# Two-column TensorE products given 128 moving columns in a two-layer hybrid backbone

## The chip, the cores and the metric

The kernel is one program on one NeuronCore of a Trainium2 chip. The metric is the device time of one execution in microseconds, from the median of several executions; lower is better. TensorE multiplies: a stationary operand of up to 128 x 128 is loaded (weight load, shown as PEld), then the moving columns stream past it (matmul, shown as PE). VectorE (DVE), ScalarE (ACT) and GpSimd (POOL) work beside it, and each engine takes its instructions in order and waits on semaphores for the others.

## What is computed

Two layers over 512 latent and 256 context tokens of width 1024, all in float32. Each layer modulates its input with vectors made from `silu(c) @ w_mod`, mixes tokens in four head groups, and ends in a squared-ReLU MLP. The three parts of the reference that the change touches:

```
m = silu_c @ w_mod[l] + b_mod[l]                       # modulation: 6 vectors of 1024, for c and for c_ctx
...
kk = heads(k * p['rwkv_k_k'][d])                       # keys of the RWKV group, 4 heads of 64, 2 directions
kk = kk / jnp.maximum(jnp.sqrt(jnp.sum(kk * kk, axis=-1, keepdims=True)), 1e-12)
...
bonus = ((jnp.sum(r * dirs[0][1] * r_k, axis=-1, keepdims=True)
          + jnp.sum(r * dirs[1][1] * r_k, axis=-1, keepdims=True)) * v)
```

## The kernel before

Features lie on the 128 partitions and tokens along the free dimension. A layer runs in order: the input projection (20 tiles), in which TensorE computes each product three times over split operands (`product`, L1460 through `mm`); attention by groups; the preparation of the RWKV group (a loop over n = 0 to 11 on TensorE); the RWKV scan in three steps of chunked products (s = 0, 1, 2), each with five levels of small 64-row products; the output projection; the MLP. Every engine's program is written out by hand, with semaphores between them, so the order on TensorE is the order of the code. All matmuls but the transposes and the scan's outputs go through the helper `mm`, so the profile gives them all line L1460.

Three kinds of products have only two moving columns. Each is float32, which the trace shows as two passes (a weight load and a matmul each) per product:

- `mod_columns(row, n, at)` (L1549) turns rows of the modulation into columns: 4n products of a 128 x 128 piece with `pick` (L133, filled once on VectorE at L999), two result columns each in PSUM bank `ps`. It runs with n = 4 at the start of a layer (from `modrow`, in L1568, or `next_row`, L1582), n = 2 after attention (L1721), n = 3 and n = 1 after the preparation (L1871, L1874), n = 2 ahead of the MLP (L2135): 48 products in layer 0 and 48 in layer 1, 96 in all. VectorE copies them to `modT` (L1093, L1098).
- The keys' square sums, in the preparation at n = 1 (L1853 to L1858): 24 products a layer of `rn` with two columns of the block matrix, `bd[:, 0:P:64]`. ScalarE takes the root (L829), VectorE the reciprocal (L1216), and TensorE spreads it over the partitions (`spread_heads`, at n = 3) after the products of n = 2 and n = 3.
- The bonus, in scan step s = 0 at level j = 2 (L1960 to L1966): 12 products a layer of `bonus_in` with the same two columns. ScalarE copies them to `bon` (L928).

`keep_clock(o, n)` issues n products of 512 columns whose result nobody reads. `spread_root` spreads a root over the partitions with products of 128 moving columns. `ring_row` computes a modulation row from four weight slabs. Unlike these, `head_sums` (L1606) has two moving columns too and is not part of the change.

Of the kernel before, what the change touches and what calls it, by code (L numbers as in the profile page):

```python
# [19 lines left out]
ALU = mybir.AluOpType  # L20
ACT = mybir.ActivationFunctionType
AX = mybir.AxisListType
# [5 lines left out]
P = 128  # L28
# [58 lines left out]
K_ID, K_ONES, K_BD, K_ROT64, K_ROT96 = range(5)  # L87
NKF = 5
# [22 lines left out]
def backbone(nc, xT_d, cT_d, pcol_d, constf_d, constm_d, rope_d, wmask_d, wmod_d, win_d, wout_d, w1_d, w2_d,  # L111
             uq_d, ukv_d, w2a2_d, g2_d, ln_d, smask_d, out_d):
    with ExitStack() as ctx:
        place = {}

        def sb(name, cols, dt=F32):
            place[name] = nc.sbuf_base
            return ctx.enter_context(nc.sbuf_tensor(name, [P, cols], dt))
# [10 lines left out]
        kf = sb("kf", NKF * P)  # L129
        km = sb("km", NKM, BF16)  # L130
        cT = sb("cT", KT * 2)
        silu = sb("silu", KT * 32)
        pick = sb("pick", 2)  # L133
        modT = sb("modT", DEPTH * NMOD * 2)
        gain = sb("gain", DEPTH * 4 * 16)
        omm = sb("omm", 32)
# [4 lines left out]
        ps = ctx.enter_context(nc.psum_tensor("ps", [P, 4096], F32))  # L141
# [5 lines left out]
        gains = gain[:, :].rearrange("p (l n k s) -> p l n k s", l=DEPTH, n=4, s=2)  # L147
        siluv = silu[:, :].rearrange("p (k m) -> p k m", k=KT)
        ident, ones, bd = (kf[:, k * P:(k + 1) * P] for k in (K_ID, K_ONES, K_BD))
        rot64 = kf[:, K_ROT64 * P:(K_ROT64 + 1) * P]  # L150
        rot96 = kf[0:96, K_ROT96 * P:K_ROT96 * P + 96]
        modrow = hT[:, 2 * SLAB:2 * SLAB + 2048]
# [59 lines left out]
        KS, BONUS = 3844, 2048 + 1024 + 256  # L212
# [5 lines left out]
        bonus_in = zv[:, R_K:R_K + 2, :]  # L218
# [3 lines left out]
        sg, aa, rn = wv(W_SG, 4, TOK), wv(W_A, 4, TOK), wv(W_RN, 4, TOK)  # L222
# [42 lines left out]
        s_silu = sem("s_silu")  # L265
# [719 lines left out]
        def _(dve):  # L985
            ch = Chain(dve, s_dve)
            V = nc.vector
# [8 lines left out]
            V.tensor_tensor(siluv[:, :, 0:2], siluv[:, :, 0:2], cT[:, :].rearrange("p (k s) -> p k s", s=2),  # L996
                            ALU.mult).then_inc(s_silu, 1)
            dve.wait_ge(s_const, 48)
            V.tensor_reduce(pick[:, :], ident.rearrange("p (q m) -> p m q", q=4)[:, 0:2, :], AX.X, ALU.add).then_inc(s_silu, 1)  # L999

            def gn_roots(n):

# [78 lines left out]
            for l in range(DEPTH):  # L1081
# [44 lines left out]
                for n, (where, tile) in enumerate(ROPES):  # L1126
                    if n >= 7:
                        dve.wait_ge(s_paire, 12 * l + n - 4)
                    p = 96 if where != 64 else P
# [3 lines left out]
                    o, at = turned_at(n), (W_VB if n < 7 else W_PT) + (n % 2) * LAT  # L1133
# [11 lines left out]
                for n, b0 in streams(l):  # L1145
# [24 lines left out]
                    with dve.Fori(0, n) as i:  # L1170
                        at = i * 12 + heads0
# [53 lines left out]
                for n in range(4):  # L1225
# [4 lines left out]
                    ins = V.tensor_tensor(kd[:, n, :], kd[:, n, :], zv[:, R_K + n % 2, :], ALU.mult)  # L1230
# [3 lines left out]
                for n in range(4):  # L1234
# [6 lines left out]
                    ins = V.tensor_tensor_scan(cs[:, n, :], smask, sg[:, n, :], 0.0, ALU.mult, ALU.add)  # L1241
                    if n >= 2:
# [4 lines left out]
                        ins = V.tensor_tensor(s3, s3, c3[:, :, CH - 1:CH].to_broadcast([P, TOK // CH, CH]), ALU.add)  # L1247
# [20 lines left out]
                for v, b in enumerate(BACKWARD):  # L1268
                    ins = V.tensor_tensor(cells(-1, RV + v * 512 + P, [64, 2], [256, 2], C1),
                                          cells(-1, R_R * TOK + b * P, [TOK, 2], [64, 2], C1),  # L1270
                                          cells(-1, 17 * TOK + b * P, [TOK, 2], [64, 2], C1), ALU.mult)
# [5 lines left out]
                for n in range(1, 3):  # L1277
                    ins = gain_of(l, n)
# [52 lines left out]
                for s in range(STEPS):  # L1331
# [13 lines left out]
                    for j, half in enumerate(LEVELS):  # L1345
                        m = M_STEP + 64 * j
# [36 lines left out]
                    for k in range(4 if s < STEPS - 1 else 3):  # L1383
                        x, i = k // 2, k % 2
# [73 lines left out]
        def _(pe):  # L1458
            def mm(out, lhsT, rhs, start=True, stop=True):
                return pe.matmul(out, lhsT, rhs, start=start, stop=stop)  # L1460
# [88 lines left out]
            def mod_columns(row, n, at):  # L1549

                for m in range(4 * n):
                    ins = mm(ps[:, at + 2 * m:at + 2 * m + 2], row[:, m * P:(m + 1) * P], pick[:, :])
                ins.then_inc(s_modps, 1)

            pe.wait_ge(s_silu, 3)
# [1 line left out]
            for l in range(DEPTH):  # L1557
# [268 lines left out]
                for n in range(12):  # L1826
                    if n == 6:
                        pe.wait_ge(s_kkn, 4 * l + 3)
                        ring_row(4)
                    if n >= 2:  # L1830
                        pe.wait_ge(s_rpe, 12 * l + n - 1)
                    o = (n % 2) * 1024
                    if n < 2:
                        for b in range(NB):
                            ins = pe.transpose(ps[:, o + b * P:o + (b + 1) * P], zv[:, R_V + n, b * P:(b + 1) * P], ident)
                    elif n < 10:
                        if n == 2:
                            pe.wait_ge(s_gate, 2 * l + 1)
                            pe.wait_ge(s_rtab, 64 * (l + 1))

                        c = (512 if n < 6 else 0) + ((n - 2) % 4) * P
                        for a, b in ((0, LAT), (LAT, TOK)):
                            ins = mm(ps[:, o + a:o + b], w2a2[:, c:c + P], zv[:, R_WA, a:b])
                    else:
                        for b in (range(4) if n == 10 else range(4, 6)):
                            c = o + (b % 4) * 256
                            mm(ps[:, c:c + 256], zv[:, R_GL, b * P:(b + 1) * P], g2a, True, False)
                            ins = mm(ps[:, c:c + 256], zv[0:32, R_MISC, b * P:(b + 1) * P], g2b, False, True)
                    ins.then_inc(s_rp, 1)
                    if n == 1:  # L1850

                        keep_clock(3072, 3)
                        pe.wait_ge(s_kkq, 4 * (l + 1))  # L1853
                        for m in range(4):
                            for b in range(NB):
                                c = KS + 12 * m + 2 * b
                                ins = mm(ps[:, c:c + 2], rn[:, m, b * P:(b + 1) * P], bd[:, 0:P:64])
                        ins.then_inc(s_kks, 1)  # L1858
                    if n == 3:

                        pe.wait_ge(s_krec, l + 1)
                        for m in range(4):
                            if m >= 2:
                                pe.wait_ge(s_kkn, 4 * l + m - 1)
                            for b in range(NB):
                                ins = spread_heads(2048 + (m % 2) * 1024 + b * P, 12 * m + 2 * b)
                            ins.then_inc(s_ksp, 1)
# [9 lines left out]
                for s in range(STEPS):  # L1877
# [69 lines left out]
                    for j, half in enumerate(LEVELS):  # L1947
                        for x in range(2):
                            h, o = HALF[x], 2048 * x
                            pe.wait_ge(s_tn[x], 6 * n + j + 1)  # L1950
                            for g in range(2):
                                for p in range(2):
                                    for f in range(2):
                                        for c in range(2):
                                            ins = mm(bank(c, o + g * P + (2 * p + f) * 32, [1, 32]),
                                                     cells(c, h + ABR + p * 512 + f * 256 + g * P, C1),
                                                     cells(c, h + TN + g * (256 + half) + (2 * p + f) * 64,
                                                           [2 * half, 32 // half], [1, half]))
                            ins.then_inc(s_X[x], 1)
                        if s == 0 and j == 2:  # L1960
                            pe.wait_ge(s_gate, 2 * l + 2)
                            for b in range(NB):
                                for f in range(2):
                                    ins = mm(ps[:, BONUS + b * 4 + 2 * f:BONUS + 2 + b * 4 + 2 * f],
                                             bonus_in[:, f, b * P:(b + 1) * P], bd[:, 0:P:64])
                            ins.then_inc(s_bonps, 1)  # L1966
                        for x in range(2):
                            h, o = HALF[x], 2048 * x + 1024
                            pe.wait_ge(s_Xm[x], 5 * n + j + 1)
                            if j == 0:  # L1970
                                pe.wait_ge(s_ke[x], n + 1)
                            else:
                                pe.wait_ge(s_tt[x], 4 * n + j)
                            if s == 0 and j == 2 and x == 1:
                                pe.wait_ge(s_bon, l + 1)
                            for g in range(2):
                                for p in range(2):
                                    for f in range(2):
                                        for c in range(2):
                                            ins = mm(bank(c, o + g * P + (2 * p + f) * 32, [1, 32]),  # L1980
                                                     cells(c, h + TT + g * 256 + (2 * p + f) * 64, C1),
                                                     cells(c, h + XM + g * P + (2 * p + f) * 32, [1, 32]))
                            ins.then_inc(s_Tp[x], 1)
                            if j == 1:
                                seen(x)
# [290 lines left out]
```

## Time and profile before

| | us |
|---|---|
| median of 3 executions | 2419.48 |
| lowest and highest | 2418.77, 2426.33 |
| span of the profiled execution | 2415.9 |
| TensorE matmul busy | 2223.2 (92%) |
| TensorE weight load busy | 1795.5 (74%) |
| VectorE, ScalarE, GpSimd busy | 1000.1, 676.1, 772.3 |
| mean granted TensorE clock | 0.955 |

The profile is of one execution, from its first to its last instruction. The granted clock is given as a share of full speed: 1.0 is 2.4 GHz, 0.5 is 1.2 GHz, and a value between is a mean over both. A matmul's duration holds its latency, so the cost of one in a series is read from where one group starts to where the next starts, divided by the count.

### The profile page before, as it was taken

The page shows a single profiled execution, that of the slowest core. Times are in us where ns is not written, and L with a number is a line of the kernel's source. Part 1 is how long each engine was busy: PE and PEld are TensorE (multiplying, and loading weights), DVE is VectorE, ACT ScalarE, POOL GpSimd, SP SyncE. Part 2 cuts the span into 40 slices and gives each one's busy share as a digit, 9 for nine tenths or more (in the row PEclk, how much of TensorE's full clock was granted, in tenths as well). Part 3 has the DMA queues.
Part 4 walks back from the last instruction along what each step waited for, and adds up shares of the span by engine and source line. Part 5 has one row for each costly group of instructions (what it writes and reads, how often), then busy time and mean ns, then how long its engine had stood idle before and what let it go on. Part 6 is the DMA issues. An engine that isn't in the chain of part 4 may idle for free.

```text
span 2415.9 us, 45856 instructions
## 1 busy us (share of the span) xinstructions
PE 2223.2 (92%) x19352; PEld 1795.5 (74%) x19352; DVE 1000.1 (41%) x1512; ACT 676.1 (28%) x1184; POOL 772.3 (32%) x546
## 2 busy tenths in 40 slices
PE   5999988889989899999999899988879988999997
PEld 3888566559966688888888578856649965888886
DVE  3002355475653732414142420335565655442443
ACT  3110455642222211102111221145642223221221
POOL 2332343013131223232222343235104133444443
PEclk9999999988999899999999899999978989999998
DMA  6211100110022211112113221110030023232331
GB/s 257 86 60 53 70 1 0 58 71 3 4 79 67 82 62 61 61 61 69 61 61 130 96 104 59 36 70 0 16 112 3 4 79 114 96 96 95 95 95 61
DMA packets 45412, 162.55 MB, mean 67 GB/s; under 512 B 5504, under 2 KB 5504, under 8 KB 45024
## 3 DMA queue, kind: packets, MB, share of 16 engines
q1 hardware_dynamic: 44480, 157.89, 19.3%
q0 software_dynamic: 800, 2.69, 0.3%
q8 instruction: 109, 1.79, 0.3%
q14 instruction: 23, 0.19, 0.0%
HBM read 158.46 MB, written 2.10 MB: 66 GB/s over the span
## 4 chain that ended last, share of the span: by engine, by line
PE 79%; DVE 13%; ACT 4%; issue 3%; POOL 1%; DMA 0%; SPq 0%; ACTq 0%; POOLq 0%; DVEq 0%
PE ps L1460 76%; DVE small L1160 2%; PE ps L1775 2%; DVE part_h L1058 1%; DVE hT L1051 1%; ACT flat L774 1%; DVE xT L1076 1%; DVE flat L1444 1%; ACT flat L792 1%; DVE ps L1157 1%; DVE flat L1074 1%; POOL flat L544 1%; PE ps L2036 0%; DVE part_h L1329 0%; DMA xT<-xT_dram 0%
## 5 line engine op out<-in xcount | busy, mean ns | idle before, releaser
L1460 PE MATMUL ps<-part_hi,wparts 128*128 128x512 f32 (+1 forms) x3072 | 825.0, 355 | 28.4 <-DVE part_h L1058 9.4
L1460 PEld LDWEIGHTS ps<-part_hi,wparts 128*128 128x128 f32 x3072 | 547.5, 191 | 120.8 <-DVE part_h L1058 15.7
L525 POOL TENSOR_TENSOR wparts<-flat,wparts 128x1024 fp32r<-128x1024 f32 x184 | 446.3, 2426 | 536.0 <-ACT wparts L974 530.3
L1460 PE MATMUL ps<-part_h,wparts 128*128 128x512 f32 (+1 forms) x1536 | 544.6, 355 | 0.0
L1460 PE MATMUL ps<-flat 64*64 64x32 f32 (+8 forms) x8812 | 491.6, 264 | 55.1 <-ACT flat L792 28.5
L1460 PEld LDWEIGHTS ps<-flat 64*64 64x64 f32 (+4 forms) x8812 | 380.1, 147 | 155.6 <-issue 75.9
L1460 PE MATMUL ps<-part_mlp,wparts 128*128 128x512 f32 (+1 forms) x1536 | 417.3, 358 | 16.2 <-DVE part_h L1058 11.3
L1460 PEld LDWEIGHTS ps<-part_h,wparts 128*128 128x128 f32 x1536 | 296.0, 193 | 39.3 <-issue 1.7
L1460 PEld LDWEIGHTS ps<-part_mlp,wparts 128*128 128x128 f32 x1536 | 275.5, 191 | 62.9 <-DVE part_h L1058 13.0
L974 ACT ACTIVATE wparts<-flat 128x1024 fp32r<-128x1024 f32 x112 | 118.8, 1061 | 705.1 <-PE ps L1460 705.1
L1460 PE MATMUL ps<-part_lo,wparts 128*128 128x512 f32 (+1 forms) x768 | 272.0, 354 | 0.0
L1444 DVE TENSOR_TENSOR flat<-flat 128x768 f32<-128x768 f32 (+1 forms) x64 | 160.2, 2503 | 213.3 <-ACT flat L978 213.1
L522 POOL CAST wparts<-flat 128x1024 fp32r<-128x1024 f32 x72 | 77.5, 1077 | 519.1 <-PE ps L1460 203.3
L1451 DVE TENSOR_TENSOR flat<-flat,ps 128x768 f32<-128x768 f32 (+1 forms) x64 | 52.6, 821 | 359.8 <-PE ps L1460 359.8
L1460 PEld LDWEIGHTS ps<-part_lo,wparts 128*128 128x128 f32 x768 | 145.3, 189 | 19.8
L1160 DVE TENSOR_REDUCE small<-ps 128x1 f32<-128x768 f32 (+2 forms) x126 | 102.1, 812 | 42.7 <-PE ps L1460 41.3
L720 ACT ACTIVATE flat<-ps 128x768 f32<-128x768 f32 (+1 forms) x40 | 30.8, 770 | 310.7 <-PE ps L1460 310.7
L774 ACT ACTIVATE flat<-ps,small 128x768 f32<-128x768 f32 (+2 forms) x126 | 98.8, 788 | 43.8 <-DVE small L1160 28.9
L1775 PE MATMUL ps<-kf,flat 128*128 128x128 f32 x592 | 91.0, 285 | 9.7 <-ACT flat L774 8.8
L1775 PEld LDWEIGHTS ps<-kf,flat 128*128 128x128 f32 x592 | 65.3, 142 | 33.6 <-issue 26.5
L1118 DVE RECIPROCAL small<-small 128x48 f32<-128x48 f32 x2 | 0.9, 452 | 210.0 <-ACT small L726 210.0
L792 ACT ACTIVATE flat<-ps 128x512 f32<-128x512 f32 (+1 forms) x120 | 63.7, 530 | 84.6 <-PE ps L1775 84.1
(202 smaller groups left out, 1953.5 us busy)
## 6 DMA issues: line engine op xcount, KB each, us to landing
flat<-w_dram SPq DMA_DIRECT2D x128, 512.0 KB, 3.5
flat<-wmod_dram SPq DMA_DIRECT2D x88, 512.0 KB, 5.5
flat<-win_dram SPq DMA_DIRECT2D x40, 512.0 KB, 3.5
flat<-wout_dram SPq DMA_DIRECT2D x16, 512.0 KB, 3.5
hT<-wmod_dram SPq DMA_DIRECT2D x8, 512.0 KB, 8.2
xT<-xT_dram SPq DMA_DIRECT2D x8, 384.0 KB, 6.1
flat<-rope_dram SPq DMA_DIRECT2D x2, 1024.0 KB, 5.7
out_dram<-xT SPq DMA_DIRECT2D x8, 256.0 KB, 2.0
```

Source lines behind the costliest of these rows:

```text
L522: ch.link(pool.tensor_copy(whi[q % 2], src))
L525: pool.tensor_tensor(wlo[q % 2], src, whi[q % 2], ALU.subtract).then_inc(s_used[q], 1)
L544: ins = pool.tensor_tensor(sq[:, 0, 0:t], sq[:, 0, 0:t], sq[:, k, 0:t], ALU.add)
L720: nc_.activation(zv[:, tile, 0:t], ps[:, (q % 2) * 1024:(q % 2) * 1024 + t], ACT.Copy).then_inc(s_ev, 1)
L774: nc_.activation(prob[:, h % 2, 0:w], ps[:, (h % 2) * 1024:(h % 2) * 1024 + w], ACT.Exp, bias=small[:, h:h + 1], accum_out=small[:, 16 + h ...
L792: nc_.activation(probT[:, h % 2, 0:w], ps[:, 2048:2048 + w], ACT.Copy).then_inc(s_pta, 1)
L974: nc_.activation(whi[q % 2], slab[:, q * SLAB:(q + 1) * SLAB], ACT.Copy).then_inc(s_whi, 1)
L1160: ins = V.tensor_reduce(nm, src, AX.X, ALU.max, negate=True)
L1444: ch.link(V.tensor_tensor(raw, raw, raw, ALU.mult))
L1451: V.tensor_tensor(yT[:, k, 0:t], yT[:, k, 0:t], ps[:, o:o + t], ALU.add).then_inc(s_ev2, 1)
L1460: return pe.matmul(out, lhsT, rhs, start=start, stop=stop)
L1775: ins = pe.transpose(ps[:, c:c + P], prob[:, h % 2, b * P:(b + 1) * P], ident)
```

## The change

The two moving columns become 128. For the modulation, `pick` is 128 wide and holds its two columns 64 times over. For the other two, `halves` reads the block matrix in the order of columns 0, 64, 1, 65 and so on, so the first two result columns are those of before. The result is written 128 columns wide at the old place; the next product starts two columns further and overwrites the surplus, and nobody reads what the last one leaves behind. The number of products and their order stay.

```diff
-        pick = sb("pick", 2)
+        pick = sb("pick", P)
...
+        halves = bd.rearrange("p (j i) -> p i j", j=2)
...
-            V.tensor_reduce(pick[:, :], ident.rearrange("p (q m) -> p m q", q=4)[:, 0:2, :], AX.X, ALU.add).then_inc(s_silu, 1)
+            V.tensor_reduce(pick[:, :].rearrange("p (i m) -> p i m", m=2),
+                            bass.AP(kf, K_ID * P, [[NKF * P, P], [0, 64], [1, 2], [32, 4]]), AX.X, ALU.add).then_inc(s_silu, 1)
...
-                    ins = mm(ps[:, at + 2 * m:at + 2 * m + 2], row[:, m * P:(m + 1) * P], pick[:, :])
+                    ins = mm(ps[:, at + 2 * m:at + 2 * m + P], row[:, m * P:(m + 1) * P], pick[:, :])
...
-                                ins = mm(ps[:, c:c + 2], rn[:, m, b * P:(b + 1) * P], bd[:, 0:P:64])
+                                ins = mm(ps[:, c:c + P], rn[:, m, b * P:(b + 1) * P], halves)
...
-                                    ins = mm(ps[:, BONUS + b * 4 + 2 * f:BONUS + 2 + b * 4 + 2 * f],
-                                             bonus_in[:, f, b * P:(b + 1) * P], bd[:, 0:P:64])
+                                    c = BONUS + b * 4 + 2 * f
+                                    ins = mm(ps[:, c:c + P], bonus_in[:, f, b * P:(b + 1) * P], halves)
```

## Rows read from the trace of the kernel before

**Rows 1.** The page: the TensorE clock over 40 slices (tenths), the chain by engine.
```profile
PEclk9999999988999899999999899999978989999998
...
PE 79%; DVE 13%; ACT 4%; issue 3%; POOL 1%; DMA 0%; SPq 0%; ACTq 0%; POOLq 0%; DVEq 0%
```

**Rows 2.** Two-column places by window: length, PE, PEld, DVE, ACT, POOL busy, clock, DMA.
```profile
37.20:41.90 4.70, 4.67 (x33) 4.68 (x34) 0.03 (x1) 0.00 (x0) 4.54 (x4) 0.78 0.60 211
134.11:136.70 2.59, 2.59 (x26) 2.59 (x25) 0.00 (x0) 1.66 (x2) 2.18 (x2) 1.00 0.00 0
...
472.80:482.76 9.96, 9.94 (x49) 9.94 (x49) 0.00 (x0) 3.11 (x4) 0.00 (x0) 0.53 0.45 177
...
551.36:554.13 2.77, 2.77 (x28) 2.75 (x24) 0.42 (x1) 0.00 (x0) 0.70 (x2) 1.00 0.00 0
...
1754.24:1762.20 7.96, 7.96 (x48) 7.96 (x49) 0.00 (x0) 3.08 (x4) 0.00 (x0) 0.66 0.51 202
```

**Rows 3.** By window as above: scan s = 0, s = 1, layer 1's s = 0.
```profile
554.13:576.72 22.59, 22.59 (x450) 22.40 (x452) 9.24 (x18) 1.39 (x3) 0.00 (x0) 0.62 0.01 2
605.19:619.99 14.80, 14.80 (x454) 14.62 (x454) 9.21 (x19) 1.20 (x2) 0.00 (x0) 1.00 0.01 3
1834.03:1856.62 22.59, 22.59 (x450) 22.41 (x453) 9.24 (x18) 1.39 (x3) 0.00 (x0) 0.62 0.01 2
555.30:570.30 15.00, 15.00 (x288) 15.00 (x286) 6.65 (x13) 0.00 (x0) 0.00 (x0) 0.50 0.01 3
```

**Rows 4.** The chain of waits around the bonus of layer 0: start, length, what.
```profile
548.95 29.79 PE ps L1460 x681
```

**Rows 5.** Timeline of TensorE in the preparation: start, length, what, count, idle before.
```profile
472.82 9.94 PE L1460 MATMUL ps<-kf,flat 128*128 128x2 f32 x48 [2.08 <-ACT flat L821]
482.62 5.00 PE L1460 MATMUL ps<-flat 128*128 128x512 f32 x8
487.55 5.49 PE L1460 MATMUL ps<-kf,small 128*64 128x128 f32 x96
492.97 2.85 PE L1460 MATMUL ps<-flat 128*128 128x512 f32 x8
...
1754.24 8.12 PE L1460 MATMUL ps<-kf,flat 128*128 128x2 f32 x48 [2.13 <-ACT flat L821]
1762.22 5.20 PE L1460 MATMUL ps<-flat 128*128 128x512 f32 x8
1767.35 5.49 PE L1460 MATMUL ps<-kf,small 128*64 128x128 f32 x96
```

**Rows 6.** Timeline as above: passes with 128 moving columns; a load between 512-column passes.
```profile
783.65 1.60 PE L1460 MATMUL ps<-kf,small 128*128 128x128 f32 x12 [0.74 <-DVE small L1026]
785.09 1.85 PE L1460 MATMUL ps<-pick,flat 128*128 128x2 f32 x16
...
1383.70 2.91 PE L1460 MATMUL ps<-kf,small 128*128 128x128 f32 x12
...
48.12 0.19 PEld L1460 LDWEIGHTS ps<-kf 128*128 128x128 f32 x1 [0.24 <-issue]
```

**Rows 7.** The chain of waits after the first modulation columns.
```profile
41.87 0.20 DVE modT L1098
...
58.85 1.07 DVE part_h L1058 x2
```

**Rows 8.** Timeline, as above, at four other places.
```profile
1386.72 2.19 DVE L1051 SCALAR_TENSOR_TENSOR hT<-xT,gain,ps 128x512 f32<-128x512 f32 x4 [0.69 <-PE ps L1460]
...
5.26 0.16 DVE L999 TENSOR_REDUCE pick<-kf 128x2 f32<-128x8 f32 x1
...
18.73 3.64 PE L1460 MATMUL ps<-flat,silu 128*32 128x512 f32 x16 [18.73 <-DMA flat<-wmod_dram]
...
531.82 1.56 PE L1460 MATMUL ps<-flat 64*64 64x128 f32 x24 [5.49 <-DVE flat L1274]
```

## The prediction

> **What bounds the kernel now.** I read the page first: the chain that ended last runs 79% on TensorE, and its clock line has slices at 7 and 8 tenths amid nines [rows 1]. So the question is which TensorE time is spent at the lower of its two clock levels, and whether the two-column products have a part in that. The second view is the table by window, laid on each two-column place [rows 2]; the third lays it on what follows the bonus and on the same work one scan step later [rows 3]; then the chain of waits and the timeline tell which of these places set the end [rows 4, 5, 7].
>
> The second view shows that a place of two-column products counts as 100% busy, yet three of the five places shown have a mean clock of 0.53 to 0.78: it falls to 1.2 GHz in the middle of them although TensorE never idles there [rows 2]. Where the clock is full, 24 passes take 2.59 us, 108 ns each; in layer 0's key sums 48 take 9.80 us, 204 ns each [rows 2, 5]. The weight load of 128 columns sets that pace: it is busy as long as the matmul is.
>
> The bonus is at full clock itself, 24 passes in 2.77 us [rows 2]. What comes right after it is not: from 555.3 to 570.3 us TensorE is 100% busy at 0.50. The stretch behind the bonus takes 22.59 us in layer 0 and the same in layer 1, and the like stretch of step s = 1, which has no bonus in it, takes 14.80 us at 1.00 with the same count of matmuls (450 against 454, some records missing) [rows 3]. So the kernel's small scan products keep a full clock that they find, and don't win back one that is lost. The chain runs through this stretch on TensorE alone [rows 4].
>
> **The change part by part.** 168 products change, 336 passes: 192 of modulation columns, 96 of key sums, 48 of bonus. Nothing is moved, and no wait is added or removed.
>
> *The price of a wider pass.* The nearest row is the spread of a root, 128 moving columns and a 128-column load: 12 passes from 783.65 to 785.09 us, 120 ns each with the start of the series in it; at half clock at most 2.91 / 12 = 243 ns [rows 6]. The lower bound is no extra cost (108 ns), as the load beside it takes as long anyway. A third row: a 512-column pass is spaced 0.19 + 0.24 = 0.43 us, so 128 columns stream in 0.11 us [rows 6]. I take 113 ns, near that streaming time, since it and the load run beside each other. The 64 passes after attention and ahead of the MLP, where the clock is full now, cost 64 x 5 ns = 0.3 us.
>
> *Bonus, each layer.* 24 x 113 ns = 2.7 us, as now. If the clock then stays, the stretch behind it is 22.59 - 14.80 = 7.8 us shorter, all on the chain: 15.6 us for both layers [rows 3, 4]. This is over half of the forecast. ScalarE's copy of the bonus and the second half's wait for it come at the same distance as before.
>
> *Key sums, each layer.* The place and the eight passes after it take 487.55 - 472.82 = 14.73 us in layer 0 and 1767.35 - 1754.24 = 13.11 us in layer 1; the like eight passes at full clock take 2.8 us [rows 5]. At full clock throughout it would be 48 x 113 ns + 2.8 = 8.2 us. In layer 1 the clock is full when the place begins and falls inside it (0.66), so I take the whole 4.9 us. In layer 0 it is low almost from the first pass (0.53), behind an idle time of 2.08 us that stays [rows 2, 5]; wide passes have to win it back. Between no fall (gain 6.5) and half of the passes at half clock (24 x 225 + 24 x 113 ns + 2.8 = 10.9 us, gain 3.8) I take 5.0. What is late next is the reciprocal on VectorE, which the spread waits for; it needs the sums, one root and two short operations, about 1.2 us behind the last product, and the 2.8 us of products cover it. Sum: 9.9 us.
>
> *First modulation columns of layer 0.* 32 passes in 4.6 us at clock 0.78 [rows 2] become 32 x 113 ns and a tail of 0.25, 3.9 us: 0.8 us less. VectorE copies right behind them, and the chain then stays with VectorE and ScalarE up to 58.85 us [rows 7]. The idle-filling products after it also come at the higher clock, but TensorE waits for VectorE there in the end, so only the 0.8 us counts.
>
> *The same in layer 1.* 1379.07 to 1383.70 us shrinks by 1.0 us. The spread of the root behind it goes from 2.91 to some 1.5 us [rows 6]. VectorE was ready 0.69 us before it [rows 8], so after the change VectorE is the late one: the gain is 1.0 + 0.69 = 1.7 us, not 2.4.
>
> *Modulation columns after the preparation.* 32 passes a layer, partly at low clock, but TensorE then idles 5.49 us for VectorE before the scan begins [rows 8]: nothing. If that cover were gone they would save about 1 us a layer.
>
> *The wider `pick`.* The reduction reads 512 elements instead of 8 in an operation that took 0.16 us at 5.26 us; the first matmul begins at 18.73 us, released by a transfer [rows 8]. Even a whole microsecond is hidden; uncovered it would cost that once.
>
> *The order in which the moving columns are read.* `pick` is read straight, the 144 passes with `halves` jump 256 bytes back and forth. No row of before reads 128 moving columns so. From below the bound is no cost. From above I take the nearest row in which a column costs four times as much streaming, the 512-column pass, 430 ns. I take no cost, because a float32 pass streams slowly: 0.83 ns a column against the 0.4 ns that its clock would allow.
>
> "Advanced Engine Details and Errata" of the Trainium skill, in its section on SBUF cachelines, speaks against this edit: a read stream that needs a new 16-byte line for every element pays a penalty, and this order does so. It gives no size; by it the 144 passes are dearer, and the time is that of the third or the fourth rival below. No run here has shown it yet.
>
> *Sum against the profiled execution.* 15.6 + 9.9 + 0.8 + 1.7 - 0.3 = 27.7 us; 2415.9 - 27.7 = 2388.2 us of span. The median stands 3.6 us above the span shown, so 2391.8, say 2392 us.
>
> **The rivals.**
> 1. *The clock doesn't depend on the columns.* The five places were at 100% busy anyway, and the clock fell for what lies around them. Then only the price is left: 336 passes x 0 to 12 ns, 2420 to 2424 us. For it speaks that two of five places keep 1.00; against it that in both layers the fall comes behind the bonus and never in the same work of s = 1 [rows 2, 3]. "TensorE: Matmul & The Clock Gate" of the Trainium skill, in its section "Why this matters for your kernels", says to keep TensorE busy without idle gaps, and the full clock will stay. By that rule alone this rival holds, since the two-column passes are back to back; the trace disagrees with it, with 0.50 right behind a stretch without idle time.
> 2. *The scan still loses its clock*, in one layer or both, because the bonus interrupts it at an unlucky moment. That gives back 7.8 or 15.6 us: 2400 or 2407 us.
> 3. *Jumping reads at half pace.* A `halves` pass takes 225 ns at full clock. The places with `halves` and what hangs on them cost 14.73 + 13.11 + 2 x (2.77 + 22.59 - 14.80) = 49.0 us now, and 144 x p + 2 x 2.8 after. With p = 0.225 they save 11.0 us, with 2.2 us of the rest 13.2: 2406 us. The clock is held all the same in this case.
> 4. *Slower: jumping reads at a quarter of the pace*, in the key sums and the bonus. With p = 0.43 the same formula gives 61.9 + 5.6 - 49.0 = 18.5 us lost, 2.2 gained: 2436 us. It decides above p = 0.316 us per pass, where 144 x p + 5.6 - 49.0 - 2.2 is zero.
> 5. *More than forecast*: layer 0's key sums never fall, passes cost 108 ns, and low stretches elsewhere shrink as well: 2378 to 2382 us.
>
> **How the numbers follow.** Chances: forecast 0.61 (2383 to 2399 us by the bounds of its terms), rival 1 0.08, rival 2 0.10, rival 3 0.10, rival 4 0.06, rival 5 0.05. The first mechanism has the same difference in two layers behind it, which is why it holds most. Low end 2382, so that the upper bound of layer 0's key sums and the cheaper pass are in; high end 2407, which takes in rivals 2 and 3 and leaves 1, 4 and part of 5 out. A measurement of this kernel can tell 0.3%, 7.3 us, from no change. Faster by more: forecast, rivals 2, 3 and 5, 0.86. Within: rival 1, 0.08. Slower: rival 4, 0.06.
>
> **What would show each step.** The stretch behind each bonus: about 14.8 us at 1.00; if it is still 22.6 at 0.62, the largest term is wrong. The key sums: 5.4 us in layer 1 and 5.4 to 8 in layer 0, and their eight followers 2.8 us. A pass with `halves` next to one with `pick` at full clock: both 110 to 120 ns, or the reads cost. The first modulation columns: 3.6 us. TensorE should still idle for VectorE ahead of the scan, longer than 5.5 us if those columns shrink. The prediction would be wrong as a whole if wide passes leave the clock where it is.

## The result, and the profile after

| | before | changed |
|---|---|---|
| median, us | 2419.12 (4 runs) | 2397.26 (4 runs, 2394.62 to 2400.76) |
| span of the profiled execution | 2415.9 | 2392.8 |
| mean granted clock | 0.955 | 0.967 |
| TensorE matmul busy | 2223.2 | 2200.9 |

The ratio of changed to before is 0.9902, with a 95% interval of 0.9882 to 0.9922: 19 to 29 us faster, 21.9 by the medians and 23.1 by the two spans. The clock has two levels, so the mean clocks say how much time is spent at the lower one: (1 - 0.955) x 2 x 2416 = 217 us before, (1 - 0.967) x 2 x 2393 = 158 us after. Line numbers of the changed kernel are one or two higher.

The table by window of the changed kernel, with the columns of rows 2, answers rows 2 and 3. The eight stretches are the first modulation columns, layer 0's key sums, layer 0's bonus, layer 1's key sums, the scan behind each bonus, layer 1's first modulation columns, and the four products of modulation columns ahead of layer 0's scan:

```profile
39.30:43.10 3.80, 3.77 (x33) 3.77 (x34) 0.00 (x0) 0.00 (x0) 3.72 (x3) 1.00 0.39 132
474.20:482.08 7.88, 7.88 (x49) 7.88 (x50) 0.00 (x0) 3.09 (x4) 0.00 (x0) 0.78 0.56 223
549.45:552.92 3.47, 3.47 (x29) 3.30 (x25) 0.43 (x1) 0.00 (x0) 0.00 (x0) 1.00 0.00 0
1743.38:1750.04 6.66, 6.66 (x48) 6.66 (x49) 0.00 (x0) 3.09 (x4) 0.00 (x0) 1.00 0.56 223
552.92:567.72 14.80, 14.80 (x449) 14.62 (x452) 8.76 (x18) 1.39 (x3) 0.00 (x0) 1.00 0.01 3
1820.10:1834.90 14.80, 14.80 (x449) 14.62 (x452) 8.76 (x18) 1.39 (x3) 0.00 (x0) 1.00 0.01 3
1369.31:1372.88 3.57, 3.57 (x34) 3.57 (x32) 2.10 (x3) 0.30 (x1) 3.49 (x3) 1.00 0.80 308
522.32:524.20 1.88, 1.88 (x8) 1.78 (x8) 1.88 (x3) 0.00 (x0) 0.00 (x0) 0.50 0.00 0
```

Behind each bonus the scan takes 14.80 us at 1.00, where it took 22.59 at 0.62 [rows 3]. The bonus itself is dearer: 3.47 us for 2.77. A pass in it costs 3.47 / 24 = 145 ns, one in layer 1's key sums 6.66 / 48 = 139 ns, both at full clock, and one of the modulation columns 3.57 / 32 = 112 ns. The first two read `halves`, the third reads `pick`.

The timeline of TensorE in the preparation answers rows 5, the eight 512- and 256-column passes among it:

```profile
474.20 8.04 PE L1462 MATMUL ps<-kf,flat 128*128 128x128 f32 x48 [2.08 <-ACT flat L822]
482.08 2.74 PE L1462 MATMUL ps<-flat 128*128 128x512 f32 x8
484.75 5.49 PE L1462 MATMUL ps<-kf,small 128*64 128x128 f32 x96
...
1743.38 6.82 PE L1462 MATMUL ps<-kf,flat 128*128 128x128 f32 x48 [2.13 <-ACT flat L822]
1750.04 2.74 PE L1462 MATMUL ps<-flat 128*128 128x512 f32 x8
1752.71 4.51 PE L1462 MATMUL ps<-kf,small 128*64 128x128 f32 x78
```

From the start of the key sums to the spread it is 10.55 us in layer 0 and 9.33 in layer 1, for 14.73 and 13.11 before: 4.2 and 3.8 us less.

### The profile page after: what moved, and what is told of

Same layout as the page of the kernel before. It is cut to its first block, busy times and chain, and to the rows that moved or that the text cites. A ratio compares the mean times of both kernels' runs of the same rounds, so it can differ in the third digit from the quotient of the medians.

```text
span 2392.8 us, 45856 instructions
## 1 busy us (share of the span) xinstructions
PE 2200.9 (92%) x19352; PEld 1772.0 (74%) x19352; DVE 998.3 (42%) x1512; ACT 675.8 (28%) x1184; POOL 772.4 (32%) x546
## 4 chain that ended last, share of the span: by engine, by line
PE 79%; DVE 13%; ACT 4%; issue 3%; DMA 1%; SPq 0%; POOL 0%; ACTq 0%; POOLq 0%; DVEq 0%
PE ps L1462 76%; DVE small L1162 2%; PE ps L1777 2%; DVE part_h L1060 1%; DVE hT L1053 1%; ACT flat L775 1%; DVE xT L1078 1%; DVE flat L1446 1%; ACT flat L793 1%; DVE ps L1159 1%; DVE flat L1076 1%; DMA flat<-wmod_dram 1%; PE ps L2038 0%; DVE part_h L1331 0%; DVE flat L1341 0%
## 5 line engine op out<-in xcount | busy, mean ns | idle before, releaser
L1462 PE MATMUL ps<-flat 64*64 64x32 f32 (+8 forms) x8812 | 474.4, 259 | 54.1 <-ACT flat L793 28.6
L1462 PEld LDWEIGHTS ps<-flat 64*64 64x64 f32 (+4 forms) x8812 | 364.7, 141 | 154.0 <-issue 75.4
L1462 PE MATMUL ps<-part_mlp,wparts 128*128 128x512 f32 (+1 forms) x1536 | 417.1, 358 | 14.6 <-DVE part_h L1060 9.7
```

## The experiments

The theory: streamed columns, not a busy engine, keep TensorE's clock; the two-column passes cost the stretches behind them their clock, each place its own. Besides it, two things were to be settled: what the `halves` passes cost and why, and whether more can be had.

### One part of the change at a time

The first three kernels keep one of the three edits of the products and take back the other two. e1 keeps the bonus:

```diff
-                    ins = mm(ps[:, at + 2 * m:at + 2 * m + P], row[:, m * P:(m + 1) * P], pick[:, :])
+                    ins = mm(ps[:, at + 2 * m:at + 2 * m + 2], row[:, m * P:(m + 1) * P], pick[:, 0:2])
...
-                                ins = mm(ps[:, c:c + P], rn[:, m, b * P:(b + 1) * P], halves)
+                                ins = mm(ps[:, c:c + 2], rn[:, m, b * P:(b + 1) * P], bd[:, 0:P:64])
```

> Only the 24 bonus products have 128 moving columns; key sums and modulation columns keep two. Theory (the two-column bonus passes cost the scan its clock, place by place): the stretch behind each bonus goes from 22.6 us at 0.62 to about 14.8 us at 1.00 in both layers, the bonus place itself from 2.8 to 3.4 us; key sums and modulation columns stay at 7.8 to 9.8 and 4.4 us. Total some 14 us below before, near 2405 us. Rival (the clock hangs on where in its program the kernel stands and on what the earlier places did): the scan of at least one layer still falls, total within 4 us of before or half of the gain.

Measured: 2402.57 us, one run, against 2417.36. e2 keeps the key sums and e3 the modulation columns, with edits of the same form.

> Only the 48 products of the keys' square sums are 128 wide. Theory: the place and its eight followers go from 14.7 and 13.1 us to about 10.6 and 9.4 us, as in the changed kernel, and the scan behind the two-column bonus still takes 22.6 us in each layer: total 7 to 8 us below before, 2411 to 2412 us. Rival (earlier places set the phase of the clock for the later ones): the scan behind the bonus keeps its clock in a layer though the bonus is untouched, and the total falls by 15 us or more.

Measured: 2407.68 us, one run.

> Only the 96 modulation products are 128 wide, read straight from pick. Theory: passes of 111 to 116 ns at full clock; the first columns of each layer take 3.6 us instead of 4.4, the four columns ahead of the scan stay as dear as the clock found there; scan stretches 22.6 us; total 1 to 3 us below before, 2416 to 2418 us. Rival: modulation columns carry a share of the scan's gain, total 8 us or more below.

Measured: 2421.93 us, one run: no gain in total. By window, first e1 (layer 0's key sums, its bonus, the scan behind it, the scan behind layer 1's bonus), then e2 (layer 0's key sums, the scan behind each bonus), then e3 (both scans):

```profile
475.00:485.16 10.16, 10.16 (x48) 10.16 (x49) 0.00 (x0) 3.09 (x4) 0.00 (x0) 0.51 0.44 174
555.00:558.47 3.47, 3.47 (x28) 3.30 (x25) 0.42 (x1) 0.00 (x0) 0.00 (x0) 1.00 0.00 0
558.47:573.27 14.80, 14.80 (x449) 14.62 (x452) 8.76 (x18) 1.39 (x3) 0.00 (x0) 1.00 0.01 3
...
1829.80:1844.60 14.80, 14.80 (x449) 14.62 (x452) 8.76 (x18) 1.39 (x3) 0.00 (x0) 1.00 0.01 3
```
```profile
473.54:480.20 6.66, 6.66 (x49) 6.66 (x49) 0.00 (x0) 3.09 (x4) 0.00 (x0) 1.00 0.62 247
549.63:572.22 22.59, 22.59 (x449) 22.41 (x452) 9.23 (x18) 1.38 (x3) 0.00 (x0) 0.62 0.01 2
...
1826.04:1848.63 22.59, 22.59 (x449) 22.41 (x452) 9.22 (x18) 1.38 (x3) 0.00 (x0) 0.62 0.01 2
```
```profile
555.01:577.60 22.59, 22.59 (x449) 22.41 (x452) 9.22 (x18) 1.39 (x3) 0.00 (x0) 0.62 0.01 2
1835.22:1857.81 22.59, 22.59 (x449) 22.40 (x452) 9.22 (x18) 1.39 (x3) 0.00 (x0) 0.62 0.01 2
```

For the scan the table is clean: a wide bonus gives 14.80 us behind it, a narrow one 22.59, in both layers of all three kernels, whatever the earlier places did. The bonus alone brings 2 x (22.59 - 14.80 - 0.7) = 14.2 us, and e1 measures 14.8. Behind the bonus the rival of a carried phase is out. At layer 0's key sums it is not: with the same wide products they take 6.66 us at 1.00 in e2 and 7.88 at 0.78 in the changed kernel, so what runs ahead of them has a part in when their clock falls. In e2, with their followers at 2.7 us, the two places save 5.4 + 3.8 = 9.2 us of the 9.7 measured. e3 was expected 1 to 3 us below before, and its one run lies 4.6 us above. One run can't tell a few us from chance, so the totals bear only the large differences here and the windows bear the rest.

### The reads of `halves`

e4 gives `halves` a tile of its own, so that the same 128 columns in the same order are read straight:

```diff
-        halves = bd.rearrange("p (j i) -> p i j", j=2)
+        halves = sb("halves", P)[:, :]
...
+            V.tensor_copy(halves.rearrange("p (i j) -> p i j", j=2), bd.rearrange("p (j i) -> p i j", j=2)).then_inc(s_silu, 1)
...
-            pe.wait_ge(s_silu, 3)
+            pe.wait_ge(s_silu, 4)
```

> The change with one thing different: halves is a tile of its own, filled once by a VectorE copy at the start with the columns in the jumping order, so TensorE reads the same 128 columns straight. Theory (the jumping read costs 28 ns a pass): bonus places fall from 3.47 to about 2.8 us, 48 key passes at full clock from 139 to about 112 ns, layer 1's key sums from 6.7 to 5.4 us, total about 4 us below the changed kernel, 2391 to 2394 us. Rival (the 28 ns come from the tiles multiplied or from what runs beside them): passes stay at 139 to 141 ns and the total equals that of the changed kernel, 2395 to 2400 us.

Measured: 2393.85 us (4 runs, 2389.17 to 2394.43), ratio to before 0.9895 (0.9874 to 0.9917). Layer 1's key sums by window:

```profile
1740.02:1745.48 5.46, 5.46 (x49) 5.46 (x49) 0.00 (x0) 3.09 (x4) 0.00 (x0) 1.00 0.71 284
```

5.46 / 48 = 114 ns, for 139: the jumping read costs 25 ns a pass, and the operands multiplied have no part in it. The totals don't tell e4 from the change: 0.9895 and 0.9902 of before, with intervals that overlap. e7 leaves the tile away and jumps still, but between the same two columns:

```diff
-        halves = bd.rearrange("p (j i) -> p i j", j=2)
+        halves = bass.AP(kf, K_BD * P, [[NKF * P, P], [0, 64], [64, 2]])
```

> The changed kernel, but halves reads the same two columns 64 times (0, 64, 0, 64 and so on) instead of 0, 64, 1, 65. It jumps 256 bytes at each column as before but touches only two places. Theory (each jump costs, wherever it lands): passes stay at 139 to 141 ns. Rival (only columns not read before cost): passes are at 112 to 116 ns as with the straight tile. The clock is held in both.

Measured: 2395.1 us, one run. Its bonus of layer 0 and key sums of layer 1:

```profile
548.29:551.16 2.87, 2.87 (x28) 2.75 (x24) 0.42 (x1) 0.00 (x0) 0.00 (x0) 1.00 0.00 0
1742.33:1747.80 5.47, 5.47 (x49) 5.47 (x50) 0.00 (x0) 3.09 (x4) 0.00 (x0) 1.00 0.67 264
```

2.87 / 24 = 120 and 5.47 / 48 = 114 ns: as with the straight tile. My theory that each jump costs has fallen. A jump of 256 bytes back and forth is free while it returns to the same two columns; it costs when it walks through new ones. Why was not tried further.

### What holds the clock in the scan

e5 has the two-column bonus again, one half at level 2 and one at level 3:

```diff
-                        if s == 0 and j == 2:
+                        if s == 0 and j in (2, 3):
...
-                            for b in range(NB):
+                            for b in range(3 * j - 6, 3 * j - 3):
```

> The changed kernel with a two-column bonus again, but half of it (6 products, 12 passes) at level 2 and half at level 3 of the scan's first step. Theory (a stretch thin in columns loses the clock): two bursts of 1.3 us with some 2 us of scan products between them are thinner than the scan alone and denser than one burst of 2.8 us; the clock holds in at least one layer and the scan behind takes about 15 us there. Rival (a two-column product as such, wherever it stands in the scan, makes the clock fall): it falls to 0.5 in both layers behind the first or the second burst and the stretch is some 7 us longer.

Measured: 2407.95 us, one run. By window, layer 0: first burst, the scan between, second burst; then layer 1's first burst and the scan behind it:

```profile
549.41:550.84 1.43, 1.43 (x16) 1.41 (x12) 0.42 (x1) 0.00 (x0) 0.58 (x2) 1.00 0.00 0
550.84:555.70 4.86, 4.86 (x130) 4.79 (x129) 2.46 (x5) 0.00 (x0) 0.00 (x0) 0.77 0.01 3
555.70:558.34 2.64, 2.64 (x14) 2.62 (x12) 0.42 (x1) 0.00 (x0) 0.00 (x0) 0.50 0.00 0
...
1822.54:1823.96 1.42, 1.42 (x15) 1.41 (x12) 0.42 (x1) 0.00 (x0) 0.54 (x1) 1.00 0.00 0
1823.96:1828.78 4.82, 4.82 (x129) 4.75 (x129) 2.46 (x5) 0.00 (x0) 0.00 (x0) 0.77 0.01 3
```

My expectation failed: 12 two-column passes, 1.43 us, were enough in both layers. The clock falls in the scan products behind the first burst, and the second burst then runs at 220 ns a pass. This result alone would also fit the rival, that a two-column product as such does the harm. e6 tells these apart. It keeps the 24 two-column passes of the bonus and puts a 128-column product, read by nobody, ahead of each of the 12 products:

```diff
-                                    ins = mm(ps[:, c:c + P], bonus_in[:, f, b * P:(b + 1) * P], halves)
+                                    mm(ps[:, BONUS + 24:BONUS + 24 + P], ident, kf[:, 0:P])
+                                    ins = mm(ps[:, c:c + 2], bonus_in[:, f, b * P:(b + 1) * P], bd[:, 0:P:64])
```

> The changed kernel with the two-column bonus again, unsplit, and ahead of each of its 12 products one product of 128 columns that nobody reads, so 48 passes instead of 24. Theory (TensorE's streamed columns hold the clock, whichever product streams them): the place takes 48 passes of about 112 ns, 5.4 us, and the stretch behind it stays at 1.00 and near 14.8 us in both layers; total about 2 us a layer above the changed kernel, near 2400 us. Rival (it is the bonus product's own form, two columns or a write of 8 bytes, that loses it): the stretch behind takes 22.6 us in both layers and the total is near 2418 us.

Measured: 2396.30 us, one run. The bonus place of layer 0, and 14.6 us behind it:

```profile
548.51:554.00 5.49, 5.49 (x54) 5.47 (x50) 0.42 (x1) 0.00 (x0) 0.50 (x1) 1.00 0.00 0
554.00:568.60 14.60, 14.60 (x443) 14.42 (x446) 8.59 (x17) 1.38 (x3) 0.00 (x0) 1.00 0.01 3
```

The two-column products are all there and the clock stays, in layer 1 too (1.00 from 1823.30 to 1837.90 us). So it is not the two-column product as such that loses it; the 128-column products streamed among them keep it, though nobody reads them. The place takes 5.49 us for the 3.47 of the change, 2 us more a layer. The total came out below the 2400 us expected, but one run can't tell so little. The fillers add columns and also break up the run of two-column passes, so these runs don't say which property of the wide products counts.

### Is more to be had

TensorE waits twice for others ahead of the scan, and 2 us ahead of the key sums. e8 is e4 with fillers there:

```diff
-                        keep_clock(3072, 3)
+                        keep_clock(3072, 5)
...
+                keep_clock(0, 3)
                 pe.wait_ge(s_prep, 5 * l + 5)
```

> The straight tile of e4, five instead of three idle-filling 512-column products ahead of the key sums, and three new ones ahead of the scan, where TensorE waits over 5 us for VectorE. Theory (what is left at the low level next to the changed places comes from TensorE's own waits): the key sums are at full clock in both layers whatever the phase, and the scan's first 128 products, partly at half clock now, take about 5.2 minus 1 to 2 us a layer: total 2 to 4 us below e4, 2388 to 2391 us. Rival (these waits are too long to be bridged, or VectorE sets the end there): within 1 us of e4 or above it, as the filler delays the scan.

Measured: 2396.59 us (4 runs, 2388.73 to 2398.34), ratio 0.9900 (0.9875 to 0.9925): not below e4. By window, a stretch of the preparation, then the scan's first 128 matmuls in both layers:

```profile
502.19:512.58 10.39, 10.38 (x29) 3.44 (x28) 5.10 (x5) 1.62 (x2) 0.00 (x0) 0.51 0.00 1
532.19:535.85 3.66, 3.66 (x129) 3.49 (x129) 3.52 (x7) 1.03 (x1) 3.63 (x7) 1.00 0.02 4
1797.87:1803.94 6.07, 6.07 (x128) 5.90 (x128) 5.04 (x9) 1.02 (x1) 6.04 (x10) 0.59 0.01 3
```

In layer 0 TensorE waited only 0.85 us behind the filler, and the 128 matmuls took 3.66 us; in layer 1 the filler ended 3.9 us before the scan, and they took 6.07. And in layer 0 the clock fell in a busy stretch, products of 256 columns at the end of the preparation, that runs at full clock in the kernel before. From 480.55 us to that fall, some 22 us, TensorE was busy without a break at 1.00 and ran no two-column pass. So thin passes are not the only thing ahead of which the clock falls, and my theory doesn't explain this fall. The columns behind it began at 513.37 us, in e4 at 507.57; of these 5.8 us e8 had 1.1 at the key sums already, so the fall cost some 4.7 us, more than the fillers could bring. This is the trace of one execution (2398.23 us); the fastest of the four took 2388.73. e9 fills both waits, four products in the first and five in the second, on top of e7:

```diff
                 mod_columns(scan_rows, 3, COL_SCAN)
+                keep_clock(0, 4)
                 ring_row(4)
...
+                keep_clock(0, 5)
                 pe.wait_ge(s_prep, 5 * l + 5)
```

> As e7 (halves reads the same two columns 64 times), with idle-filling 512-column products in TensorE's two long waits ahead of the scan: four behind the three modulation columns, five behind the one. Theory: both waits are covered, the clock is full when the scan begins in both layers, and its first 128 products take about 3.7 instead of 5.8 us: 3 to 4 us below e10, which is the same without the filler, 2388 to 2391 us. Rival (the fillers run at half clock, twice as long, and delay the scan, or the clock falls all the same): within 1 us of e10 or above it.

> The kernel of e7, timed in rounds. Theory (fresh columns of a jumping read cost 27 ns a pass, 144 passes): 3 to 4 us below e11, near 2392 us. Rival (what is saved is lost in how the clock happens to fall elsewhere): e10 and e11 within 1.5 us.

> The changed kernel again, on the same chip as e10. Both theories of the gain expect 2395 to 2400 us, 20 to 24 us below before; behind each bonus the scan takes 14.8 us in both layers again, whatever the phase of the clock.

Measured on one chip, against 2421.70 us for before:

| | median, us | lowest to highest | ratio to before |
|---|---|---|---|
| e11, the change | 2396.00 | 2394.10 to 2397.16 | 0.9898 (0.9876 to 0.9919) |
| e10, same two columns again | 2394.73 | 2390.40 to 2394.83 | 0.9885 (0.9863 to 0.9907) |
| e9, that and both waits filled | 2389.46 | 2386.84 to 2392.72 | 0.9871 (0.9845 to 0.9898) |

e11's scan takes 14.80 us behind both bonus places again. e10 lies 1.3 us below e11 with ranges that overlap: the 3.2 us which its windows show (0.8 and 1.2 in the key sums of layer 0 and 1, 0.6 in each bonus) are not shown by the total. e9 lies 6.5 us below e11, with ranges apart, and is the fastest of all. It differs from e10 by the fillers alone, and from that it lies 5.3 us below with ranges that overlap. Its first 128 scan matmuls, in layer 0 and 1:

```profile
526.93:532.25 5.32, 5.32 (x129) 5.15 (x129) 5.15 (x9) 1.02 (x1) 5.29 (x9) 0.68 0.01 3
1795.67:1799.32 3.65, 3.65 (x128) 3.48 (x129) 3.51 (x7) 1.03 (x1) 3.62 (x7) 1.00 0.02 4
```

Behind the filler TensorE waited 3.0 us for VectorE in layer 0 and 2.5 us in layer 1. In layer 0 the clock fell and little was won: the same 128 take 5.58 us in e10 (528.53 to 534.11). In layer 1 it stayed, and they take 3.65 us for 5.99 in e10 (1794.03 to 1800.02). But there the scan starts 2.6 us later behind the key sums than in e10, for the low level came in the preparation: from 1770.60 to 1780.40 us e9's clock was 0.50 and e10's 1.00. This is a second fall in a busy stretch, as in e8, and it stands ahead of the fillers that e9 adds there. The two traces cut at the same points, in us:

| stretch | e10 | e9 |
|---|---|---|
| start to layer 0's key sums | 474.52 | 474.51 |
| from there to layer 0's bonus | 74.04 | 72.20 |
| to layer 1's key sums | 1193.05 | 1193.96 |
| to layer 1's bonus | 72.86 | 73.64 |
| to the modulation columns ahead of layer 1's MLP | 196.50 | 191.27 |
| to the end | 381.93 | 381.82 |

Of the 1.8 us in layer 0, 1.6 lie in the key sums (5.47 us for 7.07), ahead of both fillers; in layer 1 the stretch with the fillers is 0.8 us longer; and 5.2 of the 5.5 us between the spans lie behind layer 1's bonus, where the two kernels are the same. So the traces don't credit the fillers with e9's lead. Its cause is open, and a difference of some 5 us between two of these kernels can come from places that no edit touches.

## Why the prediction held, and where it was off

The forecast was 2392 us in a range of 2382 to 2407, the measured median 2397.3. The mechanism was right, and the sum of 27.7 us came out at 23.1 in the span. Term by term, in us of gain:

| step | forecast | trace |
|---|---|---|
| scan behind the bonus, both layers | 15.6 | 15.6 (22.59 to 14.80, twice) |
| the bonus places themselves | 0 | -1.4 (2.77 to 3.47 us, twice) |
| key sums and their followers | 9.9 | 8.0 (4.2 + 3.8) |
| first modulation columns, layer 0 | 0.8 | 0.8 (41.70 - 37.23 to 43.01 - 39.33) |
| the same, layer 1 | 1.7 | 0.8 |
| ahead of the scan | 0 | -0.7 (layer 0's first 128 matmuls) |
| other wide passes | -0.3 | -0.3 |

The terms of the trace make 22.8 of the 23.1 us. That they meet so closely is partly luck, for differences outside the places cancel: TensorE reached the first modulation columns 2.1 us later than before (39.33 for 37.23; its first matmul, released by a transfer, came at 19.63 for 18.73), and 0.8, 0.3 and 1.3 us were won between layer 0's scan and layer 1's first columns, from there to layer 1's key sums, and behind layer 1's scan. Their cause was not followed.

*The stretch behind the bonus* was sized to a tenth of a microsecond, since the kernel did the same work once with a bonus ahead of it and once without, in one trace. e1 to e3 show the cause, and e6 that the clock stays with the two-column products still there. Rival 1, that the clock doesn't depend on the columns, is out by e1 and e6. The Trainium skill's "TensorE: Matmul & The Clock Gate", section "Why this matters for your kernels", asks for a TensorE kept busy; the trace doesn't agree that this is enough, for here it was busy throughout at 0.62 and at 1.00 alike. Rival 2 didn't occur behind the bonus in the changed kernel or in e1, e6 and e11. One sentence of the prediction is too strong: that the small products don't win back a clock that is lost. In the kernel before they did, some 17 us after the fall at 555.3 us, while the same 32-column products ran on:

```profile
571.00:572.30 1.30, 1.30 (x16) 1.30 (x14) 0.00 (x0) 0.00 (x0) 0.00 (x0) 0.50 0.00 0
572.60:576.70 4.10, 4.10 (x108) 3.92 (x108) 2.15 (x4) 1.19 (x2) 0.00 (x0) 1.00 0.00 0
```

The sum stands all the same, as it took both times from whole stretches.

*The jumping reads* are the term that I mis-sized: I took no extra cost. Against e7, which reads the same two columns again and again, the changed kernel loses 3.2 us by them: 1.2 in layer 1's key sums (6.66 for 5.47), 0.8 in layer 0's (7.88 for 7.09), where both kernels run part of the passes at half clock, and 0.6 in each bonus (3.47 for 2.87). That is 25 ns a pass at full clock, and it is the whole shortfall of the key sums (9.9 to 8.0) and 1.2 of the 1.4 us of the bonus places. Of the two bounds (0 and 320 ns) the lower was nearly right, and rival 3 (doubling) and rival 4 (fourfold, slower) were not. My reason, that a float32 pass streams slowly enough to hide it, was wrong. The trace agrees with the rule on SBUF cachelines in the Trainium skill's "Advanced Engine Details and Errata" that such a read costs, and e7 disagrees with that rule as it stands: a read that changes its line at every element costs nothing there (114 ns a pass, as straight) if it returns to the same two.

*Layer 0's key sums.* Winning the clock back was placed between 6.5 and 3.8 us of gain; it came out at 4.2. In e7, without the cost of the jumps and with a clock of 0.76 in the place, it is 9.77 us from the key sums to the spread (473.50 to 483.27), a gain of 5.0 as forecast. In e2, with jumps and no fall, it is 5.4. The half of the passes at the lower level was a guess between bounds, and what decides the fall is not known.

*Layer 1's first columns.* The step that failed is "VectorE was ready 0.69 us before": I let it move up by the 1.0 us that the columns save. TensorE did its share: the place took 3.57 us, and the spread 1.50 instead of 2.91. VectorE did not: counted from the start of the columns it was ready 6.81 us behind in the changed kernel (1376.12 - 1369.31) and 6.96 before (1386.72 - 0.69 - 1379.07), 0.15 us less and not 1.0. With the 0.69 that makes the 0.8 of the table. The timelines, first before, then the changed kernel, VectorE and GpSimd:

```profile
1383.21 2.34 POOL L525 TENSOR_TENSOR wparts<-flat,wparts 128x1024 fp32r<-128x1024 f32 x1
...
1384.11 1.50 DVE L1034 TENSOR_TENSOR modT<-modT,pcol 128x32 f32<-128x32 f32 x1
...
1385.85 0.18 DVE L1044 TENSOR_TENSOR gain<-gain,pcol 128x16 f32<-128x16 f32 x1
```

```profile
1373.31 0.33 DVE L1036 TENSOR_TENSOR modT<-modT,pcol 128x32 f32<-128x32 f32 x1
1373.67 0.17 DVE L1045 TENSOR_SCALAR gain<-modT 128x16 f32<-128x16 f32 x1
1373.88 2.20 DVE L1046 TENSOR_TENSOR gain<-gain,pcol 128x16 f32<-128x16 f32 x1
...
1376.12 2.19 DVE L1053 SCALAR_TENSOR_TENSOR hT<-xT,gain,ps 128x512 f32<-128x512 f32 x4
```
```profile
1373.67 2.38 POOL L526 TENSOR_TENSOR wparts<-flat,wparts 128x1024 fp32r<-128x1024 f32 x1
```

An operation on 16 columns takes 2.20 us, where it took 0.18 before, and ends at 1376.08, 0.03 us after GpSimd's. Before, it was L1034 that took 1.50 us and ended 0.06 us after GpSimd's; in e10 and e11 it is L1045, with 2.30 and 2.26 us, that ends 0.03 and 0.04 us after. So the next step waits for GpSimd's 2.38 us in fact, under VectorE's name: read so from four traces in which the two ends meet; no run moved GpSimd's work away.

*Ahead of the scan* I counted nothing, as TensorE waits for VectorE there. That held for its start, which came 2.8 us earlier in layer 0 (529.02 for 531.82), just as much as the key sums' followers ended. But the low level then reached further into the scan: its first 128 matmuls took 5.88 us at 0.59 in the window from 529.02 to 534.90, against 5.15 at 0.71 before. This differs between executions: in e11, the same kernel, they took 5.23 (529.63 to 534.86). The four products of modulation columns ahead (1.88 us at 0.50) are hidden by the same wait. That wait should have been longer than 5.5 us by the prediction's own sign. It was shorter, 4.62 us in layer 0 and 5.18 in layer 1, as those products ran at half clock in this trace.

*`pick`* takes 1.00 us to fill instead of 0.16, at 5.72 us, and is hidden as forecast.

## What to carry to other kernels

TensorE at 100% busy says nothing of its clock: look at the granted clock behind every burst of matmuls with few moving columns, above all where the work that follows is thin itself. Where the weight load sets the pace anyway, more moving columns are nearly free, and a wide product that nobody reads keeps the clock as a wider one does, at the price of its own time (2 us a place here). Read the surplus columns straight or repeat the same few, and trust the windows over the total when the gain is a few tenths of a per cent: they show what a place gained, and not that the whole did.

## What the runs showed of the hardware that I had not expected

- TensorE's moving read in the order 0, 64, 1, 65 costs 139 to 145 ns for 128 float32 columns, straight or as 0, 64, 0, 64 it costs 112 to 120 ns (change, e4, e7).
- A VectorE operation on 16 columns beside a GpSimd operation on 1024 ended only when that did: 2.20 us instead of 0.18 (change, e10, e11; in the kernel before it was L1034, with 1.50 us). Not every operation does: the reciprocal of 6 columns at 1381.58 us before (L1026) took 0.19 beside the GpSimd operation from 1379.81 to 1382.16.
- Behind 1.43 us of two-column passes in the scan the clock fell in both layers (e5); with a 128-column product ahead of each of the 12 two-column products of the whole bonus it stayed in both (e6).
- The clock also fell twice in a busy stretch at the end of the preparation, with no two-column pass in the 20 us ahead (e8 in layer 0, 0.51 from 502.19 to 512.58 us; e9 in layer 1, 0.50 from 1770.60 to 1780.40).
